# Moving the steps of tokens 128 to 511 to other rows of the first 128, and giving the convolution's taps a strand of their own

## What is computed

```python
hn = rms_norm(h, norm_mix_g)
xv, bg, cg, ga, gg = split(hn @ w_in)
y_sc = bg * causal_depthwise_conv(cg * xv, w_conv)                # 3 taps
u = causal_depthwise_conv(ga * sigmoid(gg), w_dw) + b_dw          # 31 taps
y_cf = silu(layer_norm(u, ln_g, ln_b))
h = h + concat(rms_norm(y_sc), rms_norm(y_cf)) @ w_out
hn = rms_norm(h, norm_ffn_g)
q = hn @ w_q                                                      # 8 heads of 256
s1, s2 = q[..., :128] @ keys[:, 0], q[..., 128:] @ keys[:, 1]
v1, i1 = top_k(s1, 16); v2, i2 = top_k(s2, 16)
vals, pos = top_k(v1[..., None] + v2[..., None, :], 16)           # expert idx, gates = softmax(vals)
act = gelu(take(u, idx) . hn)
h = h + sum((act * gates) * take(v, idx))                         # 8 heads x 16 experts a token
```

## Time and profile before

| | us |
|---|---|
| median of three runs | 2431.16 (2430.68 to 2438.27) |
| the profiled execution | 2426.73 |
| its span in the profile | 2424.9 |
| PE, DVE, ACT, POOL busy in it | 2048.5, 1768.4, 1172.8, 738.8 |
| rows 0 to 127, from the first dot to dot 128 | 116.55 to 546.7 |
| rows 128 to 255 | 546.7 to 898 |

### The profile page before, as it was taken

The page is one execution under the profiler, slowest core; times in us unless marked ns, Lnnn a source line. Parts: engine busy times, 40 slices in busy tenths (PEclk is TensorE's granted clock), DMA queues, the critical chain, the costliest instruction groups (busy, mean ns, idle before and its releaser), DMA issues. The chain is left out here.

```text
span 2424.9 us, 29683 instructions
## 1 busy us (share of the span) xinstructions
PE 2048.5 (84%) x9896; PEld 1417.0 (58%) x9896; DVE 1768.4 (73%) x3454; ACT 1172.8 (48%) x3850; POOL 738.8 (30%) x637
## 2 busy tenths in 40 slices
PE   8889887777886656999684687799989999999999
PEld 7534343333332114884342466488549978898997
DVE  6487786667778878888899988866775646656664
ACT  4354444666565564433355554433344436445443
POOL 0133343445444543333365553433320001100000
PEclk9999988899997688999895698799989999999999
DMA  8199899899999998999999999999985554224554
GB/s 356 56 364 370 357 365 353 316 390 402 416 421 399 391 408 349 388 421 421 369 400 364 381 416 420 418 401 419 421 331 202 180 176 147 87 88 157 181 184 139
DMA packets 109767, 777.72 MB, mean 321 GB/s; under 512 B 12320, under 2 KB 13088, under 8 KB 16688
## 3 DMA queue, kind: packets, MB, share of 16 engines
q0 software_dynamic: 73728, 536.90, 55.0%
q1 hardware_dynamic: 35888, 238.93, 25.8%
HBM read 773.69 MB, written 2.10 MB: 320 GB/s over the span
## 5 line engine op out<-in xcount | busy, mean ns | idle before, releaser
L2834 POOL DMA_INDIRECT pair<-in_uv,idx x512 | 620.0, 1211 | 920.2 <-DVE resid L1263 490.8
L2107 ACT ACTIVATE smalls<-smalls 128x1 f32<-128x1 f32 (+1 forms) x2058 | 540.8, 287 | 686.6 <-DVE smalls L2017 668.7
L662 PE MATMUL bank<-pair,diag 128*64 128x512 f32 (+1 forms) x1056 | 320.3, 722 | 177.7 <-ACT diag L2107 177.5
L2017 DVE CUSTOM_DVE_ANT_0 pair<-pair,hd 128x1024 f32<-128x1024 f32 x256 | 310.8, 1219 | 119.6 <-DMA pair<-in_uv,idx 118.9
L662 PE MATMUL bank<-ft,raw 128*128 128x256 f32 x1664 | 373.7, 387 | 18.5 <-DVE ft L1257 18.5
L662 PEld LDWEIGHTS bank<-ft,raw 128*128 128x128 f32 x1664 | 323.5, 195 | 64.7 <-issue 19.3
L2017 DVE CUSTOM_DVE_ANT_0 pair<-pair,hn 128x1024 f32<-128x1024 f32 x256 | 312.1, 1220 | 55.0 <-DMA pair<-in_uv,idx 54.2
L1263 DVE SCALAR_TENSOR_TENSOR resid<-pair,smalls,resid 128x1024 f32<-128x1024 f32 x243 | 310.8, 1279 | 0.7 <-ACT smalls L2107 0.6
L1257 DVE TENSOR_TENSOR half<-raw,half 128x1024 fp32r<-128x1024 f32 (+2 forms) x184 | 212.0, 1191 | 122.6 <-ACT half L2107 121.2
L662 PEld LDWEIGHTS bank<-pair,diag 128*64 128x64 f32 (+1 forms) x1056 | 77.8, 156 | 359.5 <-ACT diag L2107 241.0
L2107 ACT ACTIVATE half<-raw 128x1024 fp32r<-128x1024 f32 (+2 forms) x184 | 179.5, 1023 | 90.9 <-PE bank L662 90.8
(11 more groups left out here) (328 smaller groups left out, 3185.9 us busy)
## 6 DMA issues: line engine op xcount, KB each, us to landing
raw<-in_wts SPq DMA_DIRECT2D x199, 1024.0 KB, 8.9
pair<-in_wts SPq DMA_DIRECT2D x11, 1024.0 KB, 16.5
pair<-in_uv,idx POOLq DMA_INDIRECT x512, 10.1
raw<-in_wts SPq DMA_DIRECT2D x10, 512.0 KB, 6.3
raw<-in_wts SPq DMA_DIRECT2D x4, 720.0 KB, 6.1
resid<-in_x SPq DMA_DIRECT2D x4, 512.0 KB, 11.6
out<-resid SPq DMA_DIRECT2D x8, 256.0 KB, 5.7
raw<-in_wts SPq DMA_DIRECT2D x2, 768.0 KB, 6.5
```

Source lines behind the costliest of these rows:

```text
L662: return e.matmul(o, a, b, start=start, stop=stop)
L2017: e.tensor_tensor_reduce(b[:, 0:1024], b[:, 0:1024], x_, 1.0, 0.0, ALU.mult, ALU.add, actv[:, i % 8:i % 8 + 1]).then_inc(dotted, 1)
L2107: return e.activation(o, i, f, **kw)
L2834: e.indirect_dma_start(pair[i % NPAIR], None, uv, bass.IndirectOffsetOnAxis(ap=idx[:, n % SLOTS, k:k + 1], axis=0)).then_inc(pairs_in[i % ...
```

## The change

It changes at which row the steps of tiles 1 to 3 stand, and in which strand.

- DVE: `rest_u` from rows 1, 8, 16 to 2, 11, 19; `rest_z` from 21, 29, 33, 39 to 24, 32, 36, 42, the short convolution behind it from 2 rows later to 3; `gated_y` from 45, 47, 49, 53 to 48, 50, 52, 56; `y_mean` from 62 to 64; the six `add_tile` from 64, 65, 67, 71, 73, 75 to 66, 67, 69, 71, 76, 78.
- The taps of the long convolution get a strand of their own: one in each of rows 0 to 4 of every sixteen (where routing is), two in the others, from row 1; all done at row 69 (before: 76).
- `heads`: PE's head_q at rows 5, 19, 37, 53, 62, 76 (before 7, 23, 39, 53, 67, 75), ACT's copy 4 rows behind it (before 1), head_S 4 rows behind (before 2), its copy 7 (before 3).
- ACT: `rest_gate` at 0, 9, 17, `rest_xv` at 21, 26, 33, 39, the first taps later; squares and gained 2 rows later.
- MEAN from 78 to 70, VAR from 83 to 74. `centred` and `variance` stand 3 rows behind (before 2), `spread` at VAR + 6 (4), the squares for the variance at MEAN + 4 (3), the square root at VAR + 4 (3), silu, squares and gained at VAR + 7, 8, 9 (5, 6, 7). The bank's order is mean, var, head 7.
- `ycf` products at 82 to 92 (before 93 to 103), `hn` at 96, 100, 106 (105, 112, 115), calls from 98 and 112 on (107 and 117).
- Routing: `permute` and `lists_back` one row earlier for routings before row 128; routing 8 starts at row 112, not 114.

No operation is added or taken away. The diff, cut to changed lines and the line ahead of each:

```diff
--- before.py
+++ after.py
@@ -122,25 +122,25 @@
...
           [23, 24], [25, 26], [27], [28, 29], [30, 31]] + [[]] * 11)
-ROUTE_AT = [2 if n == 7 else 0 for n in range(32)]
+ROUTE_AT = [0] * 32
...
 TOP_ROW = {r: ROUTE_ROW[r] + 3 + LATE[r] for r in range(1, 32)}
-PERM_ROWS = {r: (ROUTE_ROW[r] + 5 + LATE[r], ROUTE_ROW[r] + 7 + LATE[r]) for r in range(1, 16)}
-BACK_ROWS = {r: (ROUTE_ROW[r] + 8 + LATE[r], ROUTE_ROW[r] + 10 + LATE[r]) for r in range(1, 16)}
+PERM_ROWS = {r: (ROUTE_ROW[r] + 4 + 2 * LATE[r], ROUTE_ROW[r] + 6 + 2 * LATE[r]) for r in range(1, 16)}
+BACK_ROWS = {r: (ROUTE_ROW[r] + 7 + 2 * LATE[r], ROUTE_ROW[r] + 9 + 2 * LATE[r]) for r in range(1, 16)}
...
               (41, 43), (43, 45), (47, 47), (49, 51)]
-Q_ROW = {2: 7, 3: 23, 4: 39, 5: 53, 6: 67, 7: 75}
-SC_SQUARES, SC_OUT = 59, [61, 63, 65, 69, 71, 73]
-MEAN, VAR = 78, 83
+Q_ROW = {2: 5, 3: 19, 4: 37, 5: 53, 6: 62, 7: 76}
+SC_SQUARES, SC_OUT = 59, [61, 63, 65, 67, 71, 73]
+MEAN, VAR = 70, 74
 CALLS = [(0, 1, 2), (1, 1, NT), (2, 1, NT), (0, 2, NT)] + [(h, 1, NT) for h in range(3, 8)]
-CALL_ROW = [107, 117, 127, 137, 147, 157, 167, 177, 187]
+CALL_ROW = [98, 112, 122, 132, 142, 152, 162, 172, 182]
@@ -198,12 +198,13 @@
...
     for c in range(8):
+        if c == 7:
+            p.add("mean", [0])
+            p.add("var", [0])
...
             p.add("ms", [0])
-    p.add("mean", [0])
-    p.add("var", [0])
@@ -216,8 +217,8 @@
...
         if c == 0:
+            p.add("hn", [6, 7, 2, 3])
             p.add("hd", [6, 7, 2, 3])
-            p.add("hn", [6, 7, 2, 3])
@@ -853,7 +854,7 @@
...
                     head_q(c, (1,))
-                    yield row + 2
+                    yield row + 4
@@ -866,31 +867,32 @@
...
                           lambda k: YTR[:, k, n % 3 * P:(n % 3 + 1) * P], 0)
+            def later():
...
                 colsum("var", 1, wide_var, REST)
...
                     for h in range(2):
-                        yield 89 + 4 * t + 2 * h
+                        yield 78 + 4 * t + 2 * h
...
                     mean_squares("mc", t, [wide_ms[t - 1]])
-                yield 105
-                turned_rows("hn", "hn", 1, HN[1])
-                yield from call(0)
+                for t, due in ((1, 96), (2, 100), (3, 106)):
+                    yield due
+                    turned_rows("hn", "hn", t, HN[t])
                 for j in range(2):
-                    yield 109 + 2 * j
+                    yield 108 + 2 * j
                     doubled(1, j)
-                yield 112
-                turned_rows("hn", "hn", 2, HN[2])
-                yield 115
-                turned_rows("hn", "hn", 3, HN[3])
-                for c in range(1, len(CALLS)):
+            def calls():
+                for c in range(len(CALLS)):
@@ -910,7 +912,7 @@
...
                     ins.then_inc(done, 1)
-                yield CALL_ROW[c] + (8 if n > P else 2)
+                yield CALL_ROW[c] + (8 if n > P else 4)
@@ -943,7 +945,7 @@
...
 
-            strands = Paced(pieces()), Paced(heads()), Paced(rest())
+            strands = Paced(pieces()), Paced(heads()), Paced(rest()), Paced(later()), Paced(calls())
@@ -1868,59 +1870,49 @@
...
 
+            def long_conv():
+                for i in range(1, MEAN):
+                    yield i
+                    pump(2 if i % 16 >= 5 else 1)
+                yield MEAN - 1
+                pump(999)
...
 
-                def conv_rows(a, b_):
-                    for i in range(a, b_):
-                        if i % 16 >= 4:
-                            yield i
-                            pump(2)
-                yield 1
-                rest_u(1)
-                yield from conv_rows(1, 8)
-                yield 8
-                rest_u(2)
-                yield from conv_rows(8, 16)
-                yield 16
-                rest_u(3)
-                row = 16
-                for ct, due in enumerate((21, 29, 33, 39)):
-                    yield from conv_rows(row, due)
+                for ct, due in ((1, 2), (2, 11), (3, 19)):
+                    yield due
+                    rest_u(ct)
+                for ct, due in enumerate((24, 32, 36, 42)):
...
                     rest_z(ct)
-                    yield from conv_rows(due, due + 2)
-                    yield due + 2
+                    yield due + 3
...
                         pass
-                    row = due + 2
-                for ct, due in enumerate((45, 47, 49, 53)):
-                    yield from conv_rows(row, due)
+                for ct, due in enumerate((48, 50, 52, 56)):
...
                     gated_y("R", 16 + ct, slice(0, REST), YTR[:, ct, :], 5 + ct)
-                    row = due
-                yield from conv_rows(row, 62)
-                yield 62
+                yield 64
                 y_mean("ms", 1, 1, 4)
-                yield 64
+                yield 66
...
                 e.wait_ge(y_rs, 3)
-                for n, due in enumerate((64, 65, 67, 71, 73, 75)):
-                    yield from conv_rows(due - 2, due)
+                for n, due in enumerate((66, 67, 69, 71, 76, 78)):
...
                     add_tile("ysc", 2 + n, t, n // 3, yrs[:, t:t + 1])
-                yield 76
-                pump(999)
-                yield MEAN + 2
+            def later():
+                yield MEAN + 3
                 centred(1, YTR[:, 4:8, :], REST)
-                yield VAR + 2
+                yield VAR + 3
                 variance(1, rstdr, REST)
-                yield VAR + 4
+                yield VAR + 6
                 spread(1, YTR[:, 4:8, :], rstdr, REST)
-                for stage, t, due in (("m", 1, 98), ("y", 1, 100), ("m", 2, 102), ("s", 1, 102), ("y", 2, 104), ("r", 1, 104),
-                                      ("s", 2, 106), ("m", 3, 106), ("r", 2, 108), ("y", 3, 108), ("s", 3, 111), ("r", 3, 113)):
+                for stage, t, due in (("m", 1, 88), ("y", 1, 90), ("m", 2, 92), ("s", 1, 93), ("y", 2, 94), ("r", 1, 95),
+                                      ("m", 3, 96), ("s", 2, 97), ("y", 3, 98), ("r", 2, 99), ("s", 3, 101), ("r", 3, 103)):
@@ -2045,7 +2037,8 @@
...
                 lists_back(0, m)
-            first, steps, between = Paced(chain("A")), iter(()), Paced(rest())
+            first, steps = Paced(chain("A")), iter(())
+            strands = Paced(rest()), Paced(later()), Paced(long_conv())
@@ -2063,7 +2056,8 @@
...
                                 lists_back(r, m)
-                    between.until(i)
+                    for strand in strands:
+                        strand.until(i)
@@ -2575,81 +2569,82 @@
...
                 for s in range(2):
-                    yield CALL_ROW[c] + (4 + 4 * s if n > P else 1)
+                    yield CALL_ROW[c] + (5 + 4 * s if n > P else 3)
...
                 for s in range(2):
-                    yield CALL_ROW[c] + (9 + s if n > P else 3)
+                    yield CALL_ROW[c] + (11 + s if n > P else 7)
...
                 for c, row in Q_ROW.items():
-                    yield row + 1
+                    yield row + 4
                     head_q(c)
-                    yield row + 3
+                    yield row + 7
...
 
-                for ct, due in ((1, 0), (2, 6), (3, 14)):
+                for ct, due in ((1, 0), (2, 9), (3, 17)):
...
                     rest_gate(ct)
-                    yield due + 1
+                    yield due + 3
                     rest_tap(ct)
-                for ct, due in enumerate((20, 28, 32, 38)):
+                for ct, due in enumerate((21, 26, 33, 39)):
...
                     rest_xv(ct)
-                    yield due + 2
+                    yield (25, 33, 37, 43)[ct]
                     rest_sc_tap(ct)
-                yield 55
+                yield 57
...
                 for t in range(3):
-                    yield 55 + t
+                    yield 57 + t // 2
...
                 for ct in range(4):
-                    yield 57 + ct // 2
+                    yield 59 + ct // 2
                     gained(YTR[:, ct, :], "g_sc", ct)
-                yield MEAN + 3
+                yield MEAN + 4
...
                     act(wide_var[ct], YTR[:, 4 + ct, :], ACT.Square).then_inc(sq_wide, 1)
-                yield VAR + 3
+                yield VAR + 4
...
                 act(rstdr, rstdr, ACT.Sqrt).then_inc(rt_wide, 1)
-                yield VAR + 5
+                yield VAR + 7
...
                     act(YTR[:, 4 + ct, :], YTR[:, 4 + ct, :], ACT.Silu, scale=col("ln_g", ct), bias=col("ln_b", ct)).then_inc(silu_cf, 1)
-                yield VAR + 6
+                yield VAR + 8
...
                     act(wide_ms[t].rearrange("p (c n) -> p c n", c=4), cubed(YTR[:, 4:8, :], t), ACT.Square).then_inc(sq_wide, 1)
-                yield VAR + 7
+                yield VAR + 9
...
                     gained(YTR[:, 4 + ct, :], "g_cf", ct)
-                yield 101
+                yield 91
                 row_squared(1)
-                yield 105
```

(23 more changed lines are left out.)

## The result

The changed kernel takes 2452.04 us in the median of seven runs, the kernel before 2431.16: a ratio of 1.0079, with a 95% interval of 1.0054 to 1.0104. It is slower by 21 us (0.8%), where 14 us less were forecast. (The ratios on record differ by less than 0.1% from the quotients of the medians.) Its profiled execution took 2449.59 us, with a span of 2447.7.

The account below looks back on a forecast made before the run. Engines waiting on each other in turns bound rows 0 to 127, transfers rows 128 to 255. Terms -14 + 2 - 2 = -14 us took the profiled 2426.73 to 2412.7, plus 4.4 to the median: 2417.0; range 2401 to 2438.

Parts of the forecast that it names:

- (f): The rest: moved calls cost 0 after row 128, permute and routing 0; rows 96 to 127 give 2 us.
- Rival 3: Slower: PE queued behind ScalarE at row 82, + 12 there against 4 gained before, 2439 us; chance 0.14.
- (c): Head 3 at row 19: PE stands 10.4 us for its weights, limiting rows 20 to 51 to 6.1 us gain.
- (e): Layer norm's chain: 4 us of waits won, + 6 for the gap around row 82, together + 2 us.
- rival 2: Swapped waits: head 3's wait and the chain take what the distances give, gain 2 us, 2429 us; chance 0.25.
- rival 1: Freed fully: head 3's wait hidden beside VectorE's routing, chain costs nothing, 30 us gained, 2401 us; chance 0.12.
- (a): Greater row distance behind PE's products: VectorE's 44 us of waits go, except at head 3's rows.
- (d): Gains of stages one to three, rows 0 to 72: 2, 5 and 7 us, together 14.
- stretch three: Third part of the first 128 rows, to row 72 or 73: bound 66.1 us by bytes, gain 7 us.
- stretch two: Rows 20 to 51: bounds 106.4 us by bytes and 103.4 by PE, gain 5 us.
- (b): Bounds of the first three stretches: at most 27.6 us; three resources within 5% never all stay full.
- Rival 4: Transfers already at their ceiling in rows 0 to 127, mean 360 GB/s; nothing won, 2431 us; chance 0.03.

Follow-up runs that it names:

- e1: The changed kernel with ScalarE's score copies of calls 1 to 8 at + 9 and + 10 rows, not + 11 and + 12: 2430.3 us, ratio 0.9983.
- e2: The kernel before with ScalarE's score copies of calls 2 to 8 at + 11 and + 12 rows, not + 9 and + 10: 2448.7 us, ratio 1.0055.
- e5: e4 with calls 1 to 8 one row later, at odd rows, and query copies at + 4 and + 8: 2406.8 us, ratio 0.9890.
- e4: e1 with head 3's query product back at row 23, not 19, its copy and scores moving with it: 2414.5 us, ratio 0.9925.
- e3: e1 with ScalarE's query copies also back, at + 4 and + 8 rows, not + 5 and + 9: 2429.8 us, ratio 0.9986.
- e11: The changed kernel with only head 3's query product back at row 23, late score copies kept: 2442.1 us, ratio 1.0040.
- e6: e4 with the six y_out products of the cf half two rows later, 84 to 94, not 82 to 92: 2403.5 us, ratio 0.9878.
- e7: e5 and e6 together, with call 0 at row 101, not 98: 2393.0 us, ratio 0.9826.
- e9: e7 with VectorE's distances back to two rows, and ScalarE's xv copies with them: 2403.4 us, ratio 0.9878.
- e10: e7 with ScalarE's head copies back at 1 and 3 rows behind the query product and PE's scores at 2: 2410.7 us, ratio 0.9911.
- e8: The kernel before with only the long convolution's taps in a strand of their own: 2437.4 us, ratio 1.0008.

## Why the prediction was wrong, step by step

**The step that failed is (f)**: that the moved calls cost 0 after row 128, as each wait of PE on ScalarE is "no more than a copy behind the pair's own diag", and the ring of seven covers it. It weighed the queries' copies (+ 9 against PE's + 8) and left out the scores' copies, which the change moves to + 11 and + 12, past the row + 10 at which the next call begins; with the plan of banks beside it, bank 0 is needed there. The transfers' share of 1.00 was taken as a reason why nothing can be lost; it is one for the opposite, as every gap there goes into the time. The wait measured 39.0 us in six, and it is worth 22 us by e1 and, in the kernel before, 13 by e2. Rows 128 to 191 took 34.9 us more than before: 27.9 of them go with this wait (e1) and 8.0 with the calls' even rows (e5 against e4), which the prediction had also set to nothing. Rival 3, "slower", named row 82 as its place: the sign was right there, the mechanism of the same kind, but most of the loss lay elsewhere. The range ended at 2438.

For the query's copies the step was right: e3 took the waits away for nothing. Waits of up to 3.9 us, as stood there, were covered; those of 9 were not. That the ring of seven is what covers them was not tried.

**The first 128 rows came out as forecast, but partly because two errors met.** The waits of (c) and (e) cost more than the sum gave them (16 us by e4, 10 by e11, and 11 by e6, where (c) lowered a bound by 6.5 and (e) took 6), and the rest of the change gained more: without them, and with call 0 at 101, rows 0 to 127 took 394.1 us in e7, 36 below the 430.2 of before. So rival 2, the swapped waits, had the mechanism right for some half of the gain, and rival 1 underrated what is there when they don't bind.

**(a) and (d), distance: the mechanism right, two sizes off.** The waits on zpad_rest, resid and yt_rest are gone: DVE's waits up to 532 us hold none of them. Rows 0 to 72 won 21.2 us, 14 were forecast. The bound by the transfers of stretch three was 66.1 us and the kernel took 62.66, at 382 GB/s; 26.9 MB in 75 us are what *before* moved in that window, and part of it belongs to later rows. So it was no bound. Nor were those of stretch two, 106.4 by bytes and 103.4 by PE: in e4 rows 20 to 51 took 98.5 us with PE busy 93.2. In that stretch PE, VectorE (92.3) and the transfers (share 1.01) were all nearly full at once, which (b) had ruled out. And the sum named VectorE's 44 us of waits as what is won; e9 puts VectorE's distance at 10 us; ScalarE's, which part (a) mentions and the sum did not count, is 18 by e10, with the reserve said there. The taps' strand was forecast at nothing and gave nothing (e8).

**(c), head 3: right.** PE stood 8.98 us for the load (10.4 forecast), 8.95 from issue to start. Its price was underrated: the step made 5 of 6.1 us the gain of rows 20 to 51 with the wait in it, and they won 7.1; without it 14.5 more by row 48 (e4). What the step left out is that VectorE waits behind PE for the routing's lists (11.94 us) and that the transfers run dry behind it (79 GB/s while head 3's products ran). The routing's steps, one row earlier and set to 0 in (f), were never put back alone.

**(e), the chain: right in every place, too small.** PE waited 8.81 us at row 82 (10 forecast), and the pairs around it ended 16.7 us apart (15.6 forecast). But rows 73 to 95 lost 8.6 us, +2 was the forecast and +12 its bound. The term mis-sized is "the difference is 8; I take +6" together with the 4 us set against it for MEAN and VAR: the gap cost 11 us by e6, VectorE's wait of 8.03 us for the routing's lists in it.

**Rival 4, the ceiling of transfers.** Excluded: rows 0 to 19 ran at 400 GB/s in the kernel after, rows 0 to 127 at 394 in e7, where the earlier trace rows has 325 to 381. The sentence of the Trainium skill, "DMA: Bandwidth & Descriptors", section "Where 436 GB/s comes from", by which the HBM side stops at about 358 GB/s a core, is not borne out here.

## What to carry to other kernels

When steps are moved in a schedule written by row, list for each bank and each buffer who frees it and who needs it next, at which rows on which engines, and compare the pairs, not only a step with its product: here a copy moved by two rows passed the next user of its bank, and six waits of 6.5 us in the mean cost 22 us, more than the change had gained by row 128. For each long wait, also list which products other engines need stand behind it on the same engine: here the routing's lists stood behind both waits before row 128. Distance between an in-order engine's product and its reader paid for both readers here, also the one whose waits look idle in a profile, as its next task feeds the loop. Where the transfers were full, waits of up to 4 us cost little or nothing, and waits of 6.4 (the longest in e2) to 9 us did cost: look at the longest wait, not only at the sum.

## What was not expected of the hardware

- A wait costs PE more than its length. The products behind the three long waits ran slower: head 3 took 6.25 us for 3.84, the first y_out 6.04 for 3.70, the call's first half product 4.94 for 2.85, 2.1 to 2.4 us each. Before each, PE had stood 8.8 to 9.0 us. The granted clock over the three was 0.59, 0.61 and 0.57, a mixture of the two levels (0.5 and 1.00), and 1.00 over head 3 in the kernel before; over rows 128 to 195 it was 0.86, and 0.97 before.
- Six waits of 39.0 us in all cost 22 us when taken away in one kernel, six of 25.7 us cost 13 when added to another: a little over half of the sum in both, and 11 us of waits on `qt` cost nothing. The sum of one kind of wait is not its price, as other waits go down when it comes up: in rows 128 to 191 the changed kernel has 39.0 us of waits on `scores`, and all of PE's waits together are 17.0 us more than before.
